# The span sums of a gated linear-attention scan: one float32 matmul each, or two rounded ones on a high and a low part

## The reference

```
def step(state, inp):                       # one chunk of 64 tokens, 4 heads, key 128
    qb, kb, vb, lfb = inp                   # lfb: log decays
    b = jnp.cumsum(lfb, axis=2)
    diff = b[:, :, :, None, :] - b[:, :, None, :, :]
    decay = jnp.where(tri, jnp.exp(jnp.where(tri, diff, 0.0)), 0.0)
    attn = jnp.einsum('bhtd,bhsd,bhtsd->bhts', qb, kb, decay)
    o = jnp.einsum('bhts,bhsv->bhtv', attn, vb) + jnp.einsum('bhtd,bhdv->bhtv', qb * jnp.exp(b), state)
    b_last = b[:, :, -1:, :]
    new_state = jnp.exp(b_last[:, :, 0, :])[..., None] * state + \
        jnp.einsum('bhsd,bhsv->bhdv', kb * jnp.exp(b_last - b), vb)
    return new_state, o
```

## Time and profile before

| | us |
|---|---|
| median of 3 runs | 6874.95 |
| lowest and highest | 6873.72, 6875.54 |
| the profiled execution, its own time | 6881.16 |
| its span, first to last instruction | 6879.5 |
| first scan (L1706 of its first chunk to its last output) | about 1944 to 2170 |
| second scan | about 3780 to 3999 |

### The profile page before, as it was taken

One profiled execution on the slowest core, in us unless ns is written; L12 is line 12 of the kernel. 1 busy time (PEld: TensorE's weight loads), 2 busy tenths in 40 slices (PEclk: granted clock), 3 DMA queues, 4 the chain that ended last, 5 costly groups with the idle time before them and its releaser, 6 DMA issues. The chain is left out here.

```text
span 6879.5 us, 96864 instructions
## 1 busy us (share of the span) xinstructions
PE 5496.4 (80%) x37796; PEld 4616.0 (67%) x37797; DVE 3018.7 (44%) x4391; ACT 2177.6 (32%) x3227; POOL 217.1 (3%) x298
## 2 busy tenths in 40 slices
PE   8837730696966796999987858859999999999994
PEld 6727610464744365999865634659898898898994
DVE  2163369543155334545522552324444454454544
ACT  2221120442132233444422213323333344444432
POOL 0010000000010000000000100010000000000000
PEclk9959965897987898999988878969999999999997
DMA  2100010012100015555420000264444445454544
GB/s 82 70 2 3 15 54 0 5 48 106 40 0 19 15 45 228 203 196 205 153 94 22 0 27 8 95 212 156 152 156 161 160 179 183 179 192 180 191 155 168
DMA packets 112625, 715.22 MB, mean 104 GB/s; under 512 B 13008, under 2 KB 16864, under 8 KB 70880
## 3 DMA queue, kind: packets, MB, share of 16 engines
q1 hardware_dynamic: 96064, 656.49, 26.3%
q0 software_dynamic: 9184, 28.49, 1.2%
q10 hardware_dynamic: 7104, 26.22, 0.9%
HBM read 639.94 MB, written 71.20 MB: 103 GB/s over the span
## 5 line engine op out<-in xcount | busy, mean ns | idle before, releaser
L2627 DVE TENSOR_TENSOR experts_low<-experts_raw,experts_high 128x1024 fp32r<-128x1024 f32 x678 | 810.9, 1224 | 1026.7 <-ACT experts_high L2556 1026.7
L2491 PE MATMUL ps<-experts_xs_high,experts_high 128*128 128x256 f32 (+1 forms) x3584 | 1039.3, 290 | 56.0 <-issue 54.9
L2491 PE MATMUL ps<-experts_xs_low,experts_high 128*128 128x256 f32 (+1 forms) x3584 | 1040.3, 290 | 0.0
L2491 PE MATMUL ps<-experts_xs_high,experts_low 128*128 128x256 f32 (+1 forms) x3584 | 1039.7, 290 | 0.0
L2491 PEld LDWEIGHTS ps<-experts_xs_high,experts_high 128*128 128x128 f32 x3584 | 683.2, 191 | 68.7 <-issue 59.3
L2556 ACT ACTIVATE experts_high<-experts_raw 128x1024 fp32r<-128x1024 f32 x678 | 687.6, 1048 | 62.8 <-DMA experts_raw<-experts 62.8
L2491 PEld LDWEIGHTS ps<-experts_xs_low,experts_high 128*128 128x128 f32 x3584 | 681.0, 190 | 9.4
L2491 PEld LDWEIGHTS ps<-experts_xs_high,experts_low 128*128 128x128 f32 x3584 | 681.8, 190 | 0.0
L2175 PE MATMUL ps<-dense_xs_parts,dense_high 128*128 128x256 f32 x2816 | 502.1, 281 | 8.4 <-issue 5.7
L2175 PEld LDWEIGHTS ps<-dense_xs_parts,dense_high 128*128 128x128 f32 x2816 | 439.0, 190 | 16.9 <-issue 9.4
L2483 PE MATMUL ps<-experts_high,experts_hid_high 128*128 128x512 f32 x1120 | 444.6, 397 | 0.0
(11 more groups left out here) (475 smaller groups left out, 9157.3 us busy)
## 6 DMA issues: line engine op xcount, KB each, us to landing
experts_raw<-experts SPq DMA_DIRECT2D x226, 1536.0 KB, 6.2
dense_raw<-dense SPq DMA_DIRECT2D x90, 1536.0 KB, 6.4
proj_raw<-w_in SPq DMA_DIRECT2D x61, 512.0 KB, 3.5
y_slot<-route_blank SPq DMA_DIRECT2D x15, 1152.0 KB, 19.8
out_proj_raw<-w_out SPq DMA_DIRECT2D x48, 256.0 KB, 2.6
spill_down<-proj_buf ACTq DMA_DIRECT2D x16, 512.0 KB, 2.6
x_mixed<-x_out SPq DMA_DIRECT2D x16, 512.0 KB, 4.7
y_slot<-experts_y ACTq DMA_DIRECT2D x8, 1024.0 KB, 9.3
```

What stands on the lines that cost most here:

```text
L2491: last = nc.tensor.matmul(ps[:, m, 0:width], w[:, u, m, c], x[:, k, 0:width], start=(k == 0 and i == 0), stop=(k == KD - 1 and i == 2))
L2627: nc.vector.tensor_tensor(low[:, v, t, :], raw[:, v % NR, t, :], high[:, v, t, :].bitcast(F32), ALU.subtract).then_inc(split, 1)
```

## The change

The decays are split into a rounded high part and a low part that holds the rest, and each head's float32 matmul becomes two rounded ones that add up in the same PSUM bank. `spans` is rounded once into a tile of its own; it holds zeros and ones. ACT makes the high part as the first instruction of `ahead(n)`, and waits for the decay copy of chunk n and, because of the two buffers, for the sums of chunk n - 2. POOL subtracts it from the decays in its own `ahead(n)`, after the decay copy and a wait for ACT. PE waits for POOL's subtraction in the place of the copy.

```
@@ gated_chunks @@
     decays = st.sb("decays", [64, 2, HALF])
+    decays_high = st.sb("decays_high", [64, 2, HALF], F32R)
+    decays_low = st.sb("decays_low", [64, 2, HALF], F32R)
+    spans = st.sb("spans", [64, HALF], F32R)
...
@@ gpsimd, ahead @@
                 pool.wait_ge(s["decays_in"], n + 1)
                 core.settle(pool)
+                pool.wait_ge(s["decays_high"], n + 1)
+                core.settle(pool)
+                nc.gpsimd.tensor_tensor(decays_low[:, u, :], decays[:, u, :], decays_high[:, u, :].bitcast(F32), ALU.subtract)\
+                    .then_inc(s["decays_split"], 1)
+                pool.wait_ge(s["decays_split"], n + 1)
+                core.settle(pool)
@@ tensor, ahead @@
-                pe.wait_ge(s["decays_in"], n + 1)
+                pe.wait_ge(s["decays_split"], n + 1)
...
                 for h in range(H):
-                    last = mm(ps[:, h, :], decays[:, u, h * P:(h + 1) * P], core.c("spans", 0, 64), start=True, stop=True)
+                    mm(ps[:, h, :], decays_high[:, u, h * P:(h + 1) * P], spans[:, :], start=True, stop=False)
+                    last = mm(ps[:, h, :], decays_low[:, u, h * P:(h + 1) * P], spans[:, :], start=False, stop=True)
@@ scalar @@
+            nc.scalar.activation(spans[:, :], core.c("spans", 0, 64), ACT.Copy).then_inc(s["spans_in"], 1)
             def ahead(n, u, i):
                 cols = bass.ds(n * CH, CH)
+                act.wait_ge(s["decays_in"], n + 1)
+                if not isinstance(n, int) or n >= 2:
+                    act.wait_ge(s["summed"], n - 1)
+                core.settle(act)
+                nc.scalar.activation(decays_high[:, u, :], decays[:, u, :], ACT.Copy).then_inc(s["decays_high"], 1)
```

More of the change, by code:

```diff
@@ L1636, in gated_chunks @@
     state = st.sb("state", [P, H, P])
-    names = ("decays_in", "value_in", "state_new", "summed", "span_exp", "q_ready", "k_ready", "raw", "k_end", "products", "masked",
+    names = ("decays_in", "decays_high", "decays_split", "spans_in", "value_in", "state_new", "summed", "span_exp", "q_ready", "k_ready", "raw", "k_end", "products", "masked",
              "attn_ready", "turned", "k_rows", "o_ready", "o_stored")
@@ L1697, in _ @@
             pe.sem_inc(s["o_ready"], 1)
+            pe.wait_ge(s["spans_in"], 1)
             def ahead(n, u, i):
-                pe.wait_ge(s["decays_in"], n + 1)
+                pe.wait_ge(s["decays_split"], n + 1)
                 if not isinstance(n, int) or n >= 1:
```

## The result

| | before | after |
|---|---|---|
| median, runs of one comparison | 6874.34 us (4 runs) | 6992.52 us (4 runs) |
| ratio to before, 95% interval | | 1.0176 [1.0158, 1.0193] |
| profiled execution, its span | 6879.5 us | 6991.4 us |

The account below looks back on a forecast made before the run. PE was taken to bound the scans: 11.81 + 3.1 stall - 1.6 sums = 13.3 us, + 2.0 for the clock = 15.3 a chunk. 26 chunks give +58.2, the ends -4: +54, so 6929 us, range 6880 to 6975.

Parts of the forecast that it names:

- The relay: Output copy, ACT's rounding, POOL's subtraction and handovers ahead of the span sums: PE stalls 3.1 us a chunk, bounds 2.4 to 3.7.
- The gain of the sums: Eight rounded span-sum matmuls instead of float32 ones save 1.6 us a chunk at full clock; 3.4 us instead of 6.8 at half.
- The rival in which the clock holds: Full clock in nearly all chunks of the scans: +2 us, 6877 us, no change; chance 0.12.
- The full-clock chunk: A scan chunk at full clock goes from 11.81 us to 13.3: 3.1 us of stall added, 1.6 us of sums saved.
- That the clock falls in each chunk: In the scans, PE's stall lets the clock fall in nearly every chunk, so the new sums cost 3.4 us instead of 1.8.
- When the clock comes back: During the score products, soon after the rounded matmuls: 0.4 us more a chunk, from a span of 0 to 2.0.
- slower still: Clock falls before the small output matmuls, returns only after the score products: about 17 us a chunk, 6973 us; chance 0.18.
- The ends: Start and end of each scan: +0.5 us at the start, -2.5 at the end, -4 us for both scans.
- The range: The whole kernel's time for 8 in 10: 6880 to 6975 us.
- the last case: The rival "slower still": about 17 us a chunk in the scans, 6973 us; chance 0.18.

Follow-up runs that it names:

- e1: The changed kernel with ACT's rounding one chunk earlier, ahead of the kt and output copies of the chunk before: 6862.4 us, ratio to before 0.9982.
- e3: The changed kernel with 22 small matmuls put on PE in its stall ahead of the span sums: 6902.0 us, ratio to before 1.0036.
- e5: The changed kernel with the same rounded matmuls over 128 input rows instead of 64, zeros in the added decay rows: 6933.0 us, ratio to before 1.0082.
- e2: The changed kernel with split and wait kept, but span sums made by the old float32 matmuls from unsplit decays: 7099.5 us, ratio to before 1.032.
- e7: The kernel of e1 with 10 small matmuls a chunk in PE's waits for kt and the attention sums: 6812.5 us, ratio to before 0.9903.
- e11: The kernel of e7 with 8 more small matmuls a chunk between span sums and score products: 6800.0 us, ratio to before 0.9891.
- e10: The kernel of e7 with the rounded matmuls over 128 rows as in e5: 6806.2 us, ratio to before 0.9901.
- e12: The edits of e10 and e11 together on the kernel of e7: 6810.0 us, ratio to before 0.9902.
- e4: The changed kernel with one more POOL copy ahead of the subtraction, stall 3.74 us instead of 3.16: 6990.1 us, ratio to before 1.0158.

## Why the prediction was right in its direction and wrong in its size

**The relay: right in its length, and in part by luck.** The prediction put 3.1 us; PE waits for 3.16 in the chunk shown. Its terms: rounding 0.63 (predicted 0.63); ACT to POOL 0.18 (0.30); POOL to PE 0.14 (0.16); the subtraction 1.50 beside DVE (1.26 plus 0.2). The 0.21 us from ACT's output copy to its rounding had no term; 0.09 us less ahead of the copy and 0.12 less from ACT to POOL made up for it. In the next chunk that gap is missing, the subtraction takes 1.81 us, and PE again waits 3.16; 1.50 and 1.81 follow each other in all later chunks. What the two chunks have in common is DVE, which goes from the key factors (L1810) to the state (L1816):

```profile
2035.97 1.95 DVE L1810 TENSOR_TENSOR gated_ks<-gated_span,qk 128x384 f32<-128x384 f32 x4
2037.84 1.11 DVE L1816 SCALAR_TENSOR_TENSOR gated_state<-gated_state,gated_span,ps 128x128 f32<-128x128 f32 x4
...
2053.13 1.96 DVE L1810 TENSOR_TENSOR gated_ks<-gated_span,qk 128x384 f32<-128x384 f32 x4
2054.40 1.81 POOL L1678 TENSOR_TENSOR gated_decays_low<-gated_decays,gated_decays_high 64x512 fp32r<-64x512 f32 x1 [11.96 <-ACT gated_decays_high L1763]
2055.00 1.12 DVE L1816 SCALAR_TENSOR_TENSOR gated_state<-gated_state,gated_span,ps 128x128 f32<-128x128 f32 x4
```

In both the subtraction ends 1.21 us after the state begins (2039.05 and 2056.21). Without key factors beside it, as in e1, it takes 1.26 us: the price by columns, taken between two other shapes, was right. So what ended last ahead of the subtraction's work was not ACT's rounding, as the prediction's sum has it, but DVE's key factors, and the subtraction's record holds the wait for them. The Trainium skill, "SBUF — State Buffer", section "Who interferes with whom", has the two engines exclude each other for the whole instruction. The records overlap here, but their ends agree with it to 0.05 us (2037.84 + 1.26 = 2039.10, 2055.00 + 1.26 = 2056.26); the prediction's reading of the earlier trace rows, that both engines slow down while they overlap, is not needed.

**The gain of the sums: right.** At half clock the sums take 3.68 us up to the products instead of 6.51. In e3, at full clock, they take 1.99 us (2036.48 to 2038.47) instead of 3.63, the 1.6 us of the prediction. The rival in which the clock holds gave +2 us for both scans; e3 has +3.4.

**The full-clock chunk: right.** 13.3 us was predicted, and with the clock held up by filler (e3) it is 13.4 to 13.5. The chunk of the earlier trace rows was the shorter of two that alternate (11.81 and 11.94), which is 0.07 of the difference.

**That the clock falls in each chunk: right.** The earlier trace rows were the proper witnesses. The Trainium skill, "TensorE: Matmul & The Clock Gate", section "HAM oscillation — how this bites in real kernels", was right to speak against the change: every chunk's batch starts slowly after its wait, with 10.24 us at half clock in each of the 26 chunks.

**When the clock comes back: wrong, and this is the miss.** Lay the chunk out in two pieces:

| from, to | before, full | predicted | measured |
|---|---|---|---|
| output copy to score products | 3.42 | 6.5 | 6.72 |
| score products to output copy | 8.39 | 8.8 | 10.45 |
| chunk | 11.81 | 15.3 | 17.17 |

The first piece holds the relay and the sums and is right to 0.2 us. The second was to be lengthened by 0.4 us, "since rounded matmuls brought the clock back soon". It was lengthened by 2.06: the products take 5.09 us instead of 3.12, and turning the keys over adds the rest. The earlier trace rows shows matmuls over 128 input rows; the scan's have 64. The prediction had named this difference itself and put "I take no difference", which held for their duration and not for what they do to the clock. e5 restores the 128 rows and in the loop changes nothing else: 15.35 us a chunk, and 52 us more than before in the scans, where the prediction had 15.3 and +54. e2 speaks against the rounding as the reason: the old float32 sums, over 64 rows too, left the products at half as well (5.02 us). In its sum, 26 x (17.09 - 15.3) = 47 of the 64 us between 6929 and the measured 6992.5 are this step alone. The rival "slower still" (about 17 us, 6973, chance 0.18) had the late return and its price in the products (2.0 us; measured 1.97). It had the clock fall ahead of the small output matmuls as well, which it did not: it fell in the wait behind them.

**The ends: wrong by 5 us.** They were to give 4 us back. The scans differ by 105.2 us, 0.5 more than the 104.7 of the 26 chunks, so the ends gave nothing: PE waits 4.37 us for the first scan's second set of sums, behind rounding and subtraction, and in the last chunk the products run at half clock after a wait of 1.99 us for the keys:

```profile
1951.92 0.76 PE L1716 MATMUL ps<-gated_spans,gated_decays_high 64*128 64x512 f32 x1 [4.37 <-POOL gated_decays_low L1678]
...
2208.77 5.52 PE L1727 MATMUL ps<-gated_qs,gated_ks 128*64 128x64 f32 x53 [1.99 <-DVE gated_ks L1810]
```

**The range.** It ended at 6975, 17 us too low. From the last case's 6973 to the measured 6992.5 it is 26 x 0.09 = 2 us of pace, 5 of the ends, 7 outside the scans and 6 by which the profiled execution was to lie above the median, which it did not after the change (6993.03 and 6992.52). Each is small; all point one way, and the range's end had room for none.

## What to carry to other kernels

Before splitting a matmul's operand on other engines, ask what their instructions stand behind in their queues: here a rounding that needed nothing of this chunk's output waited behind the output copy, and moving that one instruction (e1) was worth 130 us. Look at the neighbour as well: the subtraction got to its work only when DVE's key factors were done. A wait of PE is priced twice, by its length and by the work after it that runs at half clock; the same relay cost 3 us in the scans with work for PE in the wait (e3) and 105 without, so look at the granted clock of the stretch after the wait and not only at the idle time. When matmuls get cheaper, the waits between them weigh more; small matmuls that wait for nothing paid for themselves in those waits (e3, e7, e11), up to the point where another engine's circle sets the pace (DVE's, at 11.5 us in e10 to e12).

## What the runs showed of the hardware that was not expected

- **Input rows count for the clock's return.** Eight rounded 512-column matmuls, 3.16 us after the same wait: over 64 rows the clock was back 0.7 us before the end of the score products, over 128 rows (half of them zeros) during the last sums or 1.6 us into the products, in turn. Chunk 17.1 and 15.35 us. With the waits filled in part, 128 rows held the clock at full where 64 did not (e10 and e7, 11.5 and 12.0 us). The duration of a matmul at half clock is the same, 0.62 and 0.63 us. Why the rows count was not settled.
- **More stall, same time.** A stall 0.58 us longer changed the pace by 0.02 us (e4), since the clock came back with more of the products still to do. A price per us of stall that is read off one point does not hold beside it: in the scans -2.5 us for the first 0.58 us, +32 for the next 0.77, -15 for 0.54 less.
- **Short waits are enough.** In e1 PE's longest wait in the 13 chunks of the first scan is 1.54 us, and the clock was still at half for 3.9 us a chunk in one scan and 1.6 us in the other.
- **Unchanged code moves.** The part after the second scan lasted from 2851 (e10) to 2884 us, with the same instructions. It was not settled why.
- **VectorE and GpSimd take turns.** DVE's four query factors take 2.22 us in the change, where POOL stands still. In e1 POOL's end keys and value copies run beside such a group, and it takes 3.15 us:

```profile
2050.99 2.22 DVE L1806 TENSOR_TENSOR gated_qs<-gated_span,qk 128x448 f32<-128x448 f32 x4
```

```profile
1978.97 1.20 POOL L1689 TENSOR_TENSOR gated_ks<-gated_span,qk 128x256 f32<-128x256 f32 x1 [0.71 <-POOL gated_decays_low L1678]
1978.97 3.15 DVE L1821 TENSOR_TENSOR gated_qs<-gated_span,qk 128x448 f32<-128x448 f32 x4
```

  The end keys alone take 0.72 us (in the change at 2039.44). Moving work of POOL out of one wait put it beside DVE in another place, and there it cost the engine that sets the pace.
